# Eight late modulation chunks: products with ones against TensorE transposes and VectorE sums, with GpSimd's multiplications chained

## The reference

```python
def hybrid_layer(x, c, ...):
    mod = jax.nn.silu(c) @ ada_w + ada_b            # ada_w is 1024 x 6144, float32
    sh_m, sc_m, gt_m, sh_f, sc_f, gt_f = jnp.split(mod[:, None, :], 6, axis=-1)
    h = rms_norm(x, norm_mix) * (1 + sc_m) + sh_m
    ...                                             # mixers on h @ w_in
    x = x + gt_m * (mixed @ w_out)
    h = rms_norm(x, norm_ffn) * (1 + sc_f) + sh_f
    gate, up = jnp.split(h @ w_gate_up, 2, axis=-1)
    return x + gt_f * ((jax.nn.silu(gate) * up) @ w_down)
```

## Time and profile before

| what | value |
| --- | --- |
| median of 3 runs | 1512.59 us (1510.53 to 1513.15) |
| profiled execution: time, span | 1512.65 us, 1510.8 us |
| TensorE busy | 96% of the span |
| VectorE, ScalarE, GpSimd busy | 67%, 52%, 20% |
| mean granted TensorE clock | 0.987 of full |
| from 365 to 431 us (dn0): TensorE, VectorE, GpSimd busy | 64.7, 46.1, 54.0 of 66 us |

### The profile page before, as it was taken

The page is one execution under the profiler, slowest core; times in us unless marked ns, Lnnn a source line. Parts: engine busy times, 40 slices in busy tenths (PEclk is TensorE's granted clock), DMA queues, the critical chain, the costliest instruction groups (busy, mean ns, idle before and its releaser), DMA issues.

```text
span 1510.8 us, 28634 instructions
## 1 busy us (share of the span) xinstructions
PE 1451.1 (96%) x11986; PEld 1340.0 (89%) x11986; DVE 1015.4 (67%) x1380; ACT 790.8 (52%) x1332; POOL 309.1 (20%) x194
## 2 busy tenths in 40 slices
PE   7998999999999989999999998999999999999997
PEld 3996689999889867999998997889998998999986
DVE  1786547977667855577556787568876646588754
ACT  3774555443357545454444554466554456565642
POOL 0002313999910132068000001100000001000000
PEclk9999989999999999999999998999999999999999
DMA  9555865665654554365444732264444534345442
GB/s 385 190 198 224 292 212 217 257 229 199 247 180 172 206 228 182 112 251 196 150 169 171 272 140 84 112 223 169 170 161 181 223 135 162 112 175 198 151 176 82
DMA packets 31934, 286.73 MB, mean 190 GB/s; under 512 B 3079, under 2 KB 11559, under 8 KB 12488
## 3 DMA queue, kind: packets, MB, share of 16 engines
q1 hardware_dynamic: 27400, 266.11, 47.2%
q0 software_dynamic: 2304, 16.78, 3.0%
q10 hardware_dynamic: 2112, 2.15, 0.5%
HBM read 283.92 MB, written 7.39 MB: 193 GB/s over the span
## 4 chain that ended last, share of the span: by engine, by line
PE 76%; DVE 9%; ACT 8%; issue 3%; DMA 2%; POOL 1%; SPq 0%; POOLq 0%; DVEq 0%; ACTq 0%
PE bank L687 16%; PE bank L689 16%; PE bank L688 16%; PE bank L1179 10%; PE bank L1180 5%; PE bank L1124 2%; ACT w_hi L1559 2%; PE bank L853 1%; DVE w_lo L2121 1%; PE bank L812 1%; PE bank L826 1%; DMA ring<-ada 1%; PE bank L841 1%; PE bank L866 1%; DVE h L2079 1%
## 5 line engine op out<-in xcount | busy, mean ns | idle before, releaser
L687 PE MATMUL bank<-hi_T,w_hi 128*128 128x256 f32 x2040 | 584.5, 286 | 7.9 <-DVE mix_lo L2148 4.0
L2121 DVE TENSOR_TENSOR w_lo<-ring,w_hi 128x2048 fp32r<-128x2048 f32 (+3 forms) x215 | 481.4, 2248 | 162.7 <-ACT w_hi L1559 160.6
L689 PE MATMUL bank<-hi_T,w_lo 128*128 128x256 f32 x2040 | 578.8, 284 | 0.0
L688 PE MATMUL bank<-h_lo,w_hi 128*128 128x256 f32 x1912 | 541.3, 283 | 0.0
L1559 ACT ACTIVATE w_hi<-ring 128x2048 fp32r<-128x2048 f32 (+3 forms) x215 | 370.5, 1725 | 243.7 <-PE bank L689 109.9
L687 PEld LDWEIGHTS bank<-hi_T,w_hi 128*128 128x128 f32 x2040 | 392.3, 192 | 14.0 <-DVE mix_lo L2148 4.5
L689 PEld LDWEIGHTS bank<-hi_T,w_lo 128*128 128x128 f32 x2040 | 392.5, 192 | 0.0
L688 PEld LDWEIGHTS bank<-h_lo,w_hi 128*128 128x128 f32 x1912 | 366.7, 192 | 0.6 <-issue 0.2
L1179 PE MATMUL bank<-act_both,w_hi 128*128 128x512 f32 x672 | 238.2, 398 | 1.3 <-DVE w_lo L2121 1.3
L1180 PE MATMUL bank<-act_both,w_lo 128*128 128x256 f32 x672 | 188.5, 281 | 0.0
L1179 PEld LDWEIGHTS bank<-act_both,w_hi 128*128 128x128 f32 x672 | 126.2, 188 | 30.7 <-DVE w_lo L2121 1.6
(11 more groups left out here) (299 smaller groups left out, 1934.2 us busy)
## 6 DMA issues: line engine op xcount, KB each, us to landing
ring<-w_gu SPq DMA_DIRECT2D x22, 2048.0 KB, 7.9
ring<-w_dn SPq DMA_DIRECT2D x32, 1408.0 KB, 5.9
ring<-w_up SPq DMA_DIRECT2D x22, 2048.0 KB, 7.8
ring<-ada SPq DMA_DIRECT2D x16, 2048.0 KB, 9.0
ring<-w_mix SPq DMA_DIRECT2D x9, 2048.0 KB, 7.7
arena<-ada POOLq DMA_DIRECT2D x16, 1024.0 KB, 6.3
ring<-even_in SPq DMA_DIRECT2D x8, 2048.0 KB, 7.9
ring<-odd_in SPq DMA_DIRECT2D x6, 2048.0 KB, 7.8
```

Of the source, the lines that this page charges most:

```text
L687: nc.tensor.matmul(out, wh, xh, start=start, stop=False)
L688: nc.tensor.matmul(out, wh, xl, start=False, stop=False)
L689: return nc.tensor.matmul(out, wl, xh, start=False, stop=stop)
L2121: V.tensor_tensor(w_lo[:, n % SLOTS, at], ring[:, n % SLOTS, at], w_hi[:, u % AHEAD, 0:size].bitcast(F32), ALU.subtract).then_inc(w_lo_rea ...
```

## The change

The eight late chunks are no longer summed over partitions by products with ones. TensorE turns them instead (`turn`): four transposes of 128x128 per chunk fill a whole bank of PSUM, bank 7 for even chunks, bank 3 for chunks 13 and 15, bank 6 for 11 and 23. VectorE then sums each 128-long run with one `tensor_reduce` straight into `mod` (`turned_sum`). Two semaphores are new: `mod_turned` counts turned chunks (GpSimd waits for it before it writes a `late_sums` buffer again), `mod_added` counts summed ones (TensorE waits for it before it fills a bank again). The place of each chunk in TensorE's program stays. And GpSimd's multiplications now each wait for the one ahead (`ch(...)` in place of `ch.mark(...)`).

```diff
--- before.py
+++ after.py
@@ -157,6 +157,12 @@
     def halves_before(m):
 
         return 6 * (m // ADA_L) + m % ADA_L - ADA_FIRST
+
+    def turn_bank(m):
+
+        if m % 2 == 0:
+            return 7
+        return 3 if ADA_L <= m < ADA_L + ADA_FIRST else 6
 
     def ada_bank(m):
 
@@ -370,6 +376,8 @@
         mod_ready = sem("mod_ready")
         late_in = [sem(f"late_in{half}") for half in range(2)]
         mod_read = sem("mod_read")
+        mod_turned = sem("mod_turned")
+        mod_added = sem("mod_added")
         sq_ready = sem("sq_ready")
         sq_added = sem("sq_added")
         ssq_ready = sem("ssq_ready")
@@ -817,15 +825,23 @@
 
                 for m in range(m0, m1):
                     pe.wait_ge(acc_ready, m + 1)
+                    if m == ADA_L + ADA_FIRST:
+                        pe.wait_ge(mod_added, 2 + ADA_FIRST)
                     for t in range(4):
                         at = MOD_COL + 4 * m + t
-                        if ada_at[m] is not None:
-                            sums_m, ones = acc[:, m % 2, :], const("pick")[:, 0:1]
-                        else:
-                            sums_m, ones = late_sums[:, m % 2, :], const("ones")[:, 0:1]
-                        last = nc.tensor.matmul(bank[:, 7, at:at + 1], sums_m[:, t * P:t * P + P], ones,
+                        last = nc.tensor.matmul(bank[:, 7, at:at + 1], acc[:, m % 2, t * P:t * P + P], const("pick")[:, 0:1],
                                                 start=True, stop=True)
                     last.then_inc(mod_ready, 1)
+
+            def turn(m):
+
+                i = ada_alone.index(m)
+                pe.wait_ge(acc_ready, m + 1)
+                if i > 1:
+                    pe.wait_ge(mod_added, i - 1)
+                for t in range(4):
+                    last = nc.tensor.transpose(bank[:, turn_bank(m), t * P:t * P + P], late_sums[:, m % 2, t * P:t * P + P], ident)
+                last.then_inc(mod_turned, 1)
 
             def scores(u):
                 U = units[u]
@@ -1156,9 +1172,9 @@
                         one(j, i * (2 * SLOTS) + u0 + 2 * j + 1, i * (4 * SLOTS) + t0 + 4 * j - 3)
                 if m_next:
                     chunks(5, 6)
-                    modulations(m_next - 1, m_next)
+                    turn(m_next - 1)
                     chunks(6, 9)
-                    modulations(m_next, m_next + 1)
+                    turn(m_next)
                     chunks(9, 11)
                 else:
                     chunks(8, 11)
@@ -1187,9 +1203,9 @@
 
                     if name == "dn0" and j in NEXT_ADA:
                         m = ADA_L + NEXT_ADA.index(j)
-                        if m == ADA_L:
-                            pe.wait_ge(mod_read, 2)
-                        modulations(m, m + NEXT_ADA.count(j))
+                        pe.wait_ge(gemm_freed, ph["t0"])
+                        for late_m in range(m, m + NEXT_ADA.count(j)):
+                            turn(late_m)
 
                 pe.wait_ge(hidden_ready, done - 5)
                 part_sum(0, 0)
@@ -1585,7 +1601,7 @@
 
                 act.wait_ge(rows_ready, 2 * on_pe.index(m) + half + 1)
                 if half == 0:
-                    act.wait_ge(mod_ready, m - 1)
+                    act.wait_ge(mod_ready, on_pe.index(m) - 1)
                 nc.scalar.activation(acc[:, m % 2, half * S:half * S + S], bank[:, 7, 0:S], ACT.Copy)\
                     .then_inc(acc_ready if half else half_copied, 1)
 
@@ -2484,9 +2500,12 @@
                     low(ph["u0"] + AHEAD)
                     low(ph["u0"] + 1 + AHEAD)
                 for k in range(KT):
+                    if name == "dn0" and k in NEXT_ADA:
+                        m = ADA_L + NEXT_ADA.index(k)
+                        for late_m in range(m, m + NEXT_ADA.count(k)):
+                            turned_sum(late_m)
                     if name == "dn0" and k == KT - 1:
 
-                        dve.wait_ge(mod_ready, ADA_L + ADA_FIRST)
                         modulation(1, 0, ADA_FIRST)
                         norm_gain(1, 0).then_inc(mod_read, 2)
                         dve.wait_ge(mod_read, 4)
@@ -2537,11 +2556,24 @@
                 if r1 == 8:
                     ch(V.tensor_scalar(selm[:, qt, 0:w], work[:, 0, 0:w], -2e38, NEG, ALU.is_gt, ALU.mult))
 
+            def turned_sum(m):
+
+                dve.wait_ge(mod_turned, ada_alone.index(m) + 1)
+                at = 4 * (m % ADA_L)
+                rows = bank[:, turn_bank(m), :].rearrange("p (t n) -> p t n", t=4)
+                V.tensor_reduce(out=mod[:, m // ADA_L, at:at + 4], in_=rows, op=ALU.add, axis=AX.X).then_inc(mod_added, 1)
+
             def modulation(l, m0, m1, read=None):
 
                 at = MOD_COL + 4 * ADA_L * l
-                ins = V.tensor_tensor(mod[:, l, 4 * m0:4 * m1], bank[:, 7, at + 4 * m0:at + 4 * m1],
-                                      vec(l, "ada_b")[:, 4 * m0:4 * m1], ALU.add)
+                out, sums_m = mod[:, l, 4 * m0:4 * m1], bank[:, 7, at + 4 * m0:at + 4 * m1]
+                first, last = ADA_L * l + m0, ADA_L * l + m1 - 1
+                if first in ada_alone:
+                    sums_m = out
+                    dve.wait_ge(mod_added, ada_alone.index(last) + 1)
+                else:
+                    dve.wait_ge(mod_ready, on_pe.index(last) + 1)
+                ins = V.tensor_tensor(out, sums_m, vec(l, "ada_b")[:, 4 * m0:4 * m1], ALU.add)
                 if read:
                     ins.then_inc(read, 1)
                     dve.wait_ge(read, 2 + 3 * l)
@@ -2573,7 +2605,6 @@
                 input_columns(l)
                 mixing(l)
 
-                dve.wait_ge(mod_ready, m + 6)
                 modulation(l, ADA_FIRST, ADA_L - 2)
                 ch(norm_gain(l, 1))
                 dve.wait_ge(w_lo_ready, phases[f"out{l}"]["u0"] + AHEAD)
@@ -2613,10 +2644,12 @@
                 with dve.Fori(0, 2) as i:
                     for j in range(1, 1 + SLOTS):
                         gate_chunk(j, i)
+                turned_sum(m + 6)
                 for j in range(1 + 2 * SLOTS, 11):
                     gate_chunk(j)
-
-                dve.wait_ge(mod_ready, m + 8)
+                    if j == 8:
+                        turned_sum(m + 7)
+
                 modulation(l, ADA_L - 2, ADA_L, mod_read)
                 if l == L1 - 1:
                     dve.wait_ge(vec2_in, 16)
@@ -2859,11 +2892,11 @@
                 out = late_sums[:, m % 2, :]
                 pool.wait_ge(late_in[half], 16 * (ada_alone.index(m) + 1))
                 for k in range(k0, k0 + KT // 2):
-                    ch.mark(G.tensor_tensor(ada_late[:, k:k + 1, :], ada_late[:, k:k + 1, :],
-                                            along(c_silu[:, k:k + 1], CH), ALU.mult))
-                ch.wait()
+                    ch(G.tensor_tensor(ada_late[:, k:k + 1, :], ada_late[:, k:k + 1, :],
+                                       along(c_silu[:, k:k + 1], CH), ALU.mult))
                 if half == 0:
-                    pool.wait_ge(mod_ready, m - 1)
+                    if ada_alone.index(m) > 1:
+                        pool.wait_ge(mod_turned, ada_alone.index(m) - 1)
                     ch(G.tensor_tensor(out, ada_late[:, 0, :], ada_late[:, 1, :], ALU.add))
                 for k in range(max(k0, 2), k0 + KT // 2):
                     last = G.tensor_tensor(out, out, ada_late[:, k, :], ALU.add)
```

## The result

The changed kernel is slower: 1515.91 us (median of 20 runs, 1513.83 to 1519.41) against 1512.19 us for the kernel before (20 runs, 1507.23 to 1515.21). The ratio is 1.0027, with a 95% interval of 1.0018 to 1.0036, so 2.7 to 5.4 us. (The ratio is not the quotient of the two medians, which would be 1.0025.) The prediction was 1516.4 us.

A forecast was written before the change was run, and what follows sets the result against it. TensorE was taken to bound the kernel (76% of the span). Chunk 15 ready at 425.9 instead of 422.1 us adds 3.8 us, absorbing the 1.5 us gain, with transposes and sums 0: 1512.65 + 3.8 = 1516.4 us, range 1512.9 to 1518.8.

The forecast's parts named there:

- The main step: End of dn0: chained GpSimd finishes chunk 15 at 425.9 us, TensorE waits and goes on 3.8 us later, all reaching the end.
- Eight chunks: 0 us: TensorE, late chunks: four transposes cost the same as four products with ones, so no gain or loss over eight chunks.
- The stretch of GpSimd's run: GpSimd, chunks 10 to 15: chaining adds 3.2 us of its own time, stretched by VectorE's turns to 4.7 us.
- 28 boundaries at 0.115 us: GpSimd, chunks 10 to 15: of 36 chained boundaries 8 are hidden and 28 cost 0.115 us each, 3.2 us.
- That chunk 13 is about 3 us later stays inside its margin of 4.2 us: TensorE in dn0, near 372 us: GpSimd's later result for chunk 13 causes no wait.
- a sign of being wrong: TensorE waiting for chunk 13 near 372 us would show that GpSimd's stretch grows faster than counted.
- Two signs of being right: At chunk 15: GpSimd's last addition ends at 425 to 427 us, and TensorE is idle for 4 to 6 us ahead of it.
- The block of w_lo: VectorE's w_lo split at 382 us no longer waits for four multiplications; TensorE's stop near 385 us goes, -1.5 us.
- the hidden gaps: Rival: GpSimd's chaining gaps are mostly hidden, delay 1 to 3.8 us, net 0 to +2.9 us, centre 1514 us; chance 0.34.
- the GpSimd that is on time: Rival: GpSimd's delay at chunk 15 stays under 0.92 us and TensorE keeps its 1.48 us, 1511.2 us; chance 0.05.
- VectorE's late sums: Rival: VectorE's eight sums delay splits and through them TensorE, +5.5 us on top, 1521.9 us; chance 0.04.
- Waits for w_lo in gu0: Sign of being wrong: TensorE waiting in gu0 for w_lo; no size given.

The follow-up runs named there:

- e2: The kernel before with GpSimd's multiplications chained and nothing else changed: 1515.38 us, ratio 1.0046 to the kernel before.
- e3: The changed kernel with chunk 15 turned after output tile 7 of dn0 instead of ahead of it: 1509.67 us, ratio 0.9986 to the kernel before.
- e11: The same kernel as e3, measured again in another group: 1508.85 us, ratio 0.9979 to the kernel before.
- e1: The changed kernel with GpSimd's multiplications unchained again, so transposes and VectorE sums alone: 1512.71 us, ratio 1.0014 to the kernel before.
- e7: The changed kernel unchained, with a 128x256 matmul added on TensorE behind each late chunk's transposes: ratio 1.0000 to the kernel before.
- e10: The changed kernel, still chained, with a 128x256 matmul added on TensorE behind each chunk's transposes: ratio 1.0042 to the kernel before.
- e5: The changed kernel with only the first half of each late chunk chaining its multiplications: ratio 1.0011 to the kernel before.
- e9: The changed kernel, chained, with dn0's late chunks taken up at places 1, 3, 5 and behind tile 7: ratio 0.9988 to the kernel before.
- e6: The changed kernel with multiplications unchained and chunk 15 turned after output tile 7 of dn0: ratio 1.0009 to the kernel before.
- e8: The changed kernel unchained, with dn0's late chunks at places 1, 3, 5 and after tile 7: ratio 0.9992 to the kernel before.
- e4: The changed kernel with seven unused 128x512 matmuls on TensorE ahead of its wait for chunk 15: ratio 1.0032 to the kernel before.

## Why the prediction was right, and where it wasn't

**The main step holds.** GpSimd's chained multiplications make it late for chunk 15, TensorE stands, and the norm of layer 1 and all behind it are later. e2 shows the cause: chaining alone makes GpSimd late and the kernel slower. e3 and e11 show that the wait, with the clock behind it, is the loss: the same work with the result taken later has neither. That the number is only 0.5 us off is partly luck, as the parts below show: several were wrong, on both sides.

**The transposes were mis-sized.** "Eight chunks: 0 us" came from reading the eight records at 65.93 as four transposes. They are eight: two groups of four stand there in the code, and a transpose leaves one record where a float32 product leaves two. Four transposes take 0.36 us to the next matmul against 0.81 for four products, here at chunk 10 of the changed kernel:

```profile
304.50 0.60 PE L843 MATMUL bank<-cn,pT 128*128 128x128 f32 x4
304.86 0.37 PE L695 MATMUL bank<-hi_T,w_hi 128*128 128x256 f32 x1
```

That is 0.45 us for each chunk, 3.6 us in all. The 2.25 us of chunks 10 to 14 vanish in the wait, chunk 15's four transposes gain nothing, as they take 1.08 us at the lower clock, and 0.9 us of layer 1 stay. The figure of the Trainium skill ("TensorE: Matmul & The Clock Gate", PE-mode transpose), 275 ns for a bf16 transpose, is far above these 0.09 to 0.11 us of pitch; I read it as a latency, not a pace. The trace agrees with it as a duration: the median of the 32 transposes' records on line L843 is 0.272 us, and several are under way at once.

**The stretch of GpSimd's run was mis-sized.** 4.7 us were predicted; chaining alone gives 4.3 (e2), the whole change 6.9. The 2.6 us between are not explained: making TensorE late again took 1.7 us off the unchained run (e1 and e7), and nothing off the chained one (e10). The unit "28 boundaries at 0.115 us" is wrong as a price: half of the boundaries cost 0.4 us over e1 (e5). That the sum came out near e2's 4.3 us is the average over a run.

**"That chunk 13 is about 3 us later stays inside its margin of 4.2 us" failed.** It was 5.0 us later, and TensorE waited some 2.1 us for it. I had named this as a sign of being wrong, that the stretch grows faster than counted, and it does. Two signs of being right were missed by their size too: GpSimd ended at 427.74 us and not by 427, and TensorE's stop was 7.1 us and not 4 to 6. The wait for chunk 13 is not in the time, as the wait for chunk 15 absorbs it.

**The block of w_lo is gone**, as predicted: the longest split between 251 and 382 us takes 3.56 us, so it waited for one multiplication, against 6.29 us before, and TensorE's stop at 385 us doesn't occur. Chaining isn't needed for that each time: e1, unchained, has no such stop either. That its 1.5 us are spent in the later wait is right as well (e2 is 1.5 us ahead of before at 395 us, and 6.4 us behind at the end of dn0). By the Trainium skill ("SBUF — State Buffer", on the engine ports) one instruction holds the shared ports; that VectorE is kept out by unchained multiplications for all four is what the traces show, though not each time (before, at 407 us, a split got in behind the first).

**Not foreseen: the clock.** The prediction has no term for it. A stop of 7.1 us was followed by 5.6 us of work at 1.2 GHz, by my estimate some 2.7 us lost. The end of dn0 is 7.9 us late and not 3.8. In the profiled execution most of that came back: 4.4 us between 540 and 620 us, where the clock in the mixers of layer 1 was higher than before, 0.9 us by layer 1's transposes, and 1.0 us more by 1200 us. It ended only 1.4 us above the one of before, for which 3.8 us were forecast. The medians differ by 3.7 us; how that divides between dn0 and the clock elsewhere no trace shows, as one execution of each was profiled. So the 0.5 us between 1516.4 and 1515.91 flatter the sum: on the side of loss GpSimd's stretch was too small and the clock left out, on the side of gain the transposes and the clock of layer 1 were left out.

**Of the rivals**, the hidden gaps and the GpSimd that is on time fell (427.74 us for 425.9 predicted). VectorE's late sums fell by e7: the eight reductions take 0.68 us each, and the time shows none of it. Waits for w_lo in gu0 did not appear.

## What to carry to other kernels

Where a slow helper engine works in one unbroken run towards a fixed place in the main engine's program, find the margin at each of these places before you touch either: here 0.9 us in 170, and each improvement ahead of the place (faster transposes, no w_lo block) went into the wait. Move the place before you tune the work: taking one result 7.8 us later turned +0.27% into -0.14 to -0.21%. Then find the margin anew: at the new place it was 0.6 us, and the next gain ahead of it (e9) was spent in a wait again. And look at operands that move from PSUM to SBUF on an engine that takes turns with another: an 8-column addition went from 0.15 to 1.26 us, and to 4.50 us beside unchained multiplications.

## What the runs showed of the hardware

- Four unchained multiplications of GpSimd often kept a VectorE tensor_tensor with both inputs in SBUF out until all four were done (before: six groups of twelve, for up to 4.1 us). In the other groups VectorE got in between. With 0.08 us between them VectorE got in after one (the longest split between 251 and 382 us is 3.56 us against 6.29). Chaining lengthened GpSimd's run by 4.3 us in 170. TensorE waited 1.3 to 3.3 us for w_lo in dn0 in four of the five unchained kernels (before, e6, e7, e8; not in e1), and in the chained ones only in e9, for 0.9 us.
- TensorE's granted clock fell to 1.2 GHz behind stops of 4.5 to 7.1 us at chunk 15, in e1, e2, e5, e10 and the changed kernel, and didn't there in e4, where seven matmuls whose results nobody uses filled the stop. It also fell behind a stop of 2.6 us in e8, but not behind one of 3.3 us in e6. In the mixers of layer 1 the mean clock was 0.98 to 0.92 in the kernels with a half clock at chunk 15 and 0.96 to 0.89 in those without. Why stretches at the lower level come and go there isn't explained by these runs.
- Executions of one kernel differ by up to 12.7 us (e6: 1504.51 to 1517.22 us). The start alone, up to gu0, differed by -2.7 to +2.6 us from before between profiled executions, which is why the table counts from gu0.
